# A transformer forward kernel on one core: four small transfers change queue and the mixer around them is re-ordered; the first feed-forward entry is re-cut

## What is computed

```
x = x + sliding_window_sink_attention(rms_norm(x, norm_mix), ...)
x = x + swiglu_ffn(rms_norm(x, norm_ffn), w_gate_up, w_down)      # silu(h @ gate) * (h @ up) @ down
x = rms_norm(x, final_norm)
# the plain mixer, ab_mixer(rms_norm(x, ab_norm)):
p = h @ w_in                       # qk | va | oa | gates (16 columns) | uv
qk = silu(centred_dwconv(qk, conv_w))            # five taps along the sequence
g = gates + gate_b                 # log_i, log_sigmoid(forget), forward and backward
h_fwd, h_bwd = mlstm_scan(q, k, v, ...)          # decay rows from cumulative sums and maxima of g
u, vb = split(gelu(uv));  vb = rms_norm(vb);  hb = u * (ws @ vb + bs)
out = concat(rms_norm(h_fwd + h_bwd) * sigmoid(oa), hb) @ w_out
```

## Time and profile before

| | |
|---|---|
| median of 3 runs | 880.72 us (879.99 to 880.95) |
| the profiled execution | 878.9 us, span 877.2 us |
| TensorE busy | 858.1 us, 98% of the span |
| VectorE, ScalarE, GpSimd busy | 541.6, 434.5, 48.1 us |
| chain that ended last | 92% TensorE, 4% VectorE |
| mean granted TensorE clock | 0.994 |

### The profile page before, as it was taken

How to read it: one execution, slowest core, us unless ns; L and a number is a source line. 1 busy time by engine, 2 the same in 40 slices (tenths; PEclk the granted TensorE clock), 3 DMA queues, 4 the chain that set the end, 5 groups by cost and what they waited for, 6 DMA issues and landing times.

```text
span 877.2 us, 14208 instructions
## 1 busy us (share of the span) xinstructions
PE 858.1 (98%) x5784; PEld 774.5 (88%) x5784; DVE 541.6 (62%) x590; ACT 434.5 (50%) x595; POOL 48.1 (5%) x113
## 2 busy tenths in 40 slices
PE   8999999999999989999999999999999999999996
PEld 8977899999998988889999999999867999999995
DVE  5897554444448669777765555567576675555553
ACT  6675443343344785553744444436465364444431
POOL 2200000000001100310000000003000000000000
PEclk9999999999999998999999999999999999999999
DMA  9644355545555655337575555453602576555601
GB/s 314 226 155 147 121 182 190 193 156 191 188 192 148 221 164 174 115 98 216 177 247 183 184 187 189 135 169 105 230 1 91 195 229 195 181 184 183 190 38 49
DMA packets 98442, 147.68 MB, mean 168 GB/s; under 512 B 4042, under 2 KB 81938, under 8 KB 98402
## 3 DMA queue, kind: packets, MB, share of 16 engines
q1 hardware_dynamic: 97234, 143.11, 50.0%
q0 software_dynamic: 1120, 4.00, 1.6%
q10 hardware_dynamic: 48, 0.02, 0.0%
HBM read 146.05 MB, written 1.05 MB: 168 GB/s over the span
## 4 chain that ended last, share of the span: by engine, by line
PE 92%; DVE 4%; ACT 1%; POOL 1%; issue 1%; DMA 1%; ACTq 0%; DVEq 0%; POOLq 0%
PE bank L1921 28%; PE bank L1922 27%; PE bank L1923 27%; PE bank L1992 1%; PE bank L2579 1%; PE bank L2602 1%; PE bank L2564 1%; PE bank L2558 1%; PE bank L2121 1%; PE bank L2140 1%; DMA x_norm<-arena 1%; DVE w_lo L1209 1%; PE bank L2332 0%; PE bank L2304 0%; PE bank L2044 0%
## 5 line engine op out<-in xcount | busy, mean ns | idle before, releaser
L1209 DVE TENSOR_TENSOR w_lo<-w_raw,w_hi 128x2048 fp32r<-128x2048 f32 (+3 forms) x129 | 289.5, 2252 | 150.9 <-ACT w_hi L682 150.7
L1921 PE MATMUL bank<-xT_hi,w_hi 128*128 128x256 f32 x1068 | 306.0, 286 | 4.3 <-DVE w_lo L1209 4.2
L1923 PE MATMUL bank<-xT_hi,w_lo 128*128 128x256 f32 x1068 | 304.0, 285 | 0.0
L1922 PE MATMUL bank<-xT_lo,w_hi 128*128 128x256 f32 x1068 | 304.0, 285 | 0.0
L682 ACT ACTIVATE w_hi<-w_raw 128x2048 fp32r<-128x2048 f32 (+3 forms) x129 | 241.2, 1877 | 92.4 <-PE bank L1923 85.2
L1921 PEld LDWEIGHTS bank<-xT_hi,w_hi 128*128 128x128 f32 x1068 | 205.6, 192 | 9.3 <-DVE w_lo L1209 4.4
L1922 PEld LDWEIGHTS bank<-xT_lo,w_hi 128*128 128x128 f32 x1068 | 205.7, 193 | 1.9 <-issue 0.2
L1923 PEld LDWEIGHTS bank<-xT_hi,w_lo 128*128 128x128 f32 x1068 | 205.6, 193 | 0.2
L1921 PE MATMUL bank<-w_hi,ff_hi 128*128 128x512 f32 x344 | 134.8, 392 | 0.0
L1922 PE MATMUL bank<-w_lo,ff_hi 128*128 128x512 f32 x344 | 134.5, 391 | 0.0
L1923 PE MATMUL bank<-w_hi,ff_lo 128*128 128x512 f32 x344 | 134.0, 390 | 0.0
(11 more groups left out here) (269 smaller groups left out, 768.6 us busy)
## 6 DMA issues: line engine op xcount, KB each, us to landing
w_raw<-in_ffn_w SPq DMA_DIRECT2D x64, 1024.0 KB, 5.4
w_raw<-in_ffn_w_gate_up SPq DMA_DIRECT2D x22, 1024.0 KB, 5.1
w_raw<-in_ab_w_in SPq DMA_DIRECT2D x12, 1024.0 KB, 6.1
w_raw<-in_ffn_w_down SPq DMA_DIRECT2D x11, 1024.0 KB, 5.0
w_raw<-in_swa_w_in SPq DMA_DIRECT2D x5, 1024.0 KB, 10.9
w_raw<-in_swa_w_out SPq DMA_DIRECT2D x4, 1024.0 KB, 6.3
w_raw<-in_ab_w_out SPq DMA_DIRECT2D x4, 1024.0 KB, 4.9
w_raw<-in_c_w_out SPq DMA_DIRECT2D x4, 1024.0 KB, 6.6
```

The costliest lines, as they stand in the source:

```text
L1209: dve.tensor_tensor(view(w_lo, ch), view(w_raw, ch), view(w_hi, ch).bitcast(F32), ALU.subtract).then_inc(S["lo_done"], 1)
L1921: pe.matmul(out, sh, mh, start=first, stop=False)
L1922: pe.matmul(out, sh, ml, start=False, stop=False)
L1923: return pe.matmul(out, sl, mh, start=False, stop=last)
```

## The change

In the plain mixer the four gate-row transfers are issued by POOL. ACT takes the second half of vb right after the first and rounds C7 and C8 in one go. DVE subtracts C5 to C8 in one go before it waits for the gate rows, does `conv(0)` ahead of `gate_rows`, and spreads C9 to C12 anew. ACT's Exp and Ln move behind its copies of P5.

In the first feed-forward entry DVE subtracts the second chunk in two halves, one ahead of each `normalise`; both row-tile-0 halves are transposed and lowered in one step; T1 is done in halves inside the second visit; and the pieces of the output projection change places, so that the bank of tile 0 ends one piece earlier.

```
+            pool.wait_ge(S["g_raw_ready"], 1)
+            for k in range(4):
+                pool.dma_start(g4[:, k, :], g_raw[4 * k:4 * k + 4, :]).then_inc(S["g4_loaded"], 16)
...
                 sum_squares(n, 0)
-                transposed_high(use, 0, (0,))
-                sum_squares(n, 1, (0,))
-                transposed_high(use, 0, (1,))
-                sum_squares(n, 1, (1,))
-                high_upto(early)
+                transposed_high(use, 0)
+                sum_squares(n, 1)
                 transposed_high(use, 1)
...
             spatial_values(0)
-            act.wait_ge(S["mm_done"], c[3].index + 1)
+            spatial_values(1)
             high_upto(c[6].index + 1)
...
-            act.wait_ge(S["g_raw_ready"], 1)
-            for k in range(4):
-                act.dma_start(g4[:, k, :], g_raw[4 * k:4 * k + 4, :]).then_inc(S["g4_loaded"], 16)
             act.wait_ge(S["pads_ready"], 1)
             act.wait_ge(S["params_ready"], 1)
-            high_upto(c[7].index + 1)
-            spatial_values(1)
-            act.wait_ge(S["g_abs_ready"], 1)
-            step(act.activation(g_w, g_w, ACT.Exp))
-            act.activation(g_w, g_w, ACT.Ln, bias=1.0).then_inc(S["g_ln_ready"], 1)
+            high_upto(c[8].index + 1)
...
+            def enter(use, n, second, then):
+                def part(half):
+                    dve.wait_ge(S["hi_done"], second.index + 1)
+                    k = slice(4 * half, 4 * half + 4)
+                    return dve.tensor_tensor(view(w_lo, second)[:, k], view(w_raw, second)[:, k],
+                                             view(w_hi, second)[:, k].bitcast(F32), ALU.subtract)
...
                 add_residual(n, 0)
-                low_upto(early)
+                part(0)
                 normalise(n, 0, x_norm)
                 add_residual(n, 1, (0,))
-                transposed_low(use, 0, (0,))
+                transposed_low(use, 0)
                 add_residual(n, 1, (1,))
-                transposed_low(use, 0, (1,))
+                part(1).then_inc(S["lo_done"], 1)
+                split[0] += 1
                 normalise(n, 1, x_norm)
...
-            low_upto(c[6].index + 1)
+            low_upto(c[8].index + 1)
...
-            low_upto(c[7].index + 1)
+            conv(0)
...
             gate_rows()
-            for i in range(4):
-                conv(i)
-                low_upto(c[min(8 + i, 10)].index + 1)
+            low_upto(c[9].index + 1)
+            conv(1)
+            low_upto(c[10].index + 1)
...
-            low_upto(c[8].index + 1 + SLOTS)
+            conv(2)
+            conv(3)
+            low_upto(c[11].index + 1)
...
             weighted_scores(1)
+            low_upto(c[12].index + 1)
...
+            swa_values(3)
             out_part(2, 0, 0)
-            swa_values(3)
             out_part(2, 0, 1)
-            out_part(2, 1, 0)
             out_part(3, 0, 0)
             out_part(3, 0, 1)
+            out_part(2, 1, 0)
             out_part(2, 1, 1)
...
-            enter(1, 1, [by_tile(c[0], halves(0)), by_tile(c[1], halves(1))])
+            first, second = by_tile(c[0], halves(0)), by_tile(c[1], halves(1))
+            first(0, low_count=4 + 1)
+            second(0, at=((4, lambda: transpose_tile(1, 1, (0,))), (6, lambda: transpose_tile(1, 1, (1,)))))
+            first(1, low_count=4 + 3)
+            second(1)
```

More of the change, by code:

```diff
@@ L722, in transposed_high, with enter @@
                                    bank[2 * t + half][:], ACT.Copy).then_inc(S["xTh_ready"], 1)
-            def enter(use, n, early, then):
+            def enter(use, n, then):
                 sum_squares(n, 0)
-                transposed_high(use, 0, (0,))
-                sum_squares(n, 1, (0,))
-                transposed_high(use, 0, (1,))
-                sum_squares(n, 1, (1,))
-                high_upto(early)
+                transposed_high(use, 0)
+                sum_squares(n, 1)
                 transposed_high(use, 1)
@@ L833, in _ @@
             c = sched["ffn1"]
-            enter(1, 1, 0, c[3].index + 1)
+            enter(1, 1, c[3].index + 1)
             def silu_gate(ch, i, it=0):
@@ L958, in _ @@
                 last.then_inc(S["conv_begun"], 1)
+                if i == 0:
+                    act.wait_ge(S["g_abs_ready"], 1)
+                    step(act.activation(g_w, g_w, ACT.Exp))
+                    act.activation(g_w, g_w, ACT.Ln, bias=1.0).then_inc(S["g_ln_ready"], 1)
                 high_upto(ch.index + 1 + SLOTS)
@@ L1467, in first_hidden_low @@
                                   ff_hi[0][:].bitcast(F32), ALU.subtract).then_inc(S[ready], 1)
-            enter(1, 1, c[1].index + 1, c[3].index + 1)
+            enter(1, 1, c[1], c[3].index + 1)
             dve.wait_ge(S["ff1_sg"], 1)
```

## The result

The changed kernel takes 869.51 us (median of 4 runs, 868.01 to 869.93); the kernel before, measured beside it, 880.36 us (878.09 to 880.95). The ratio is 0.9878, 95% interval 0.9857 to 0.9900. The prediction said 872.7 us, with a range of 870.8 to 876.5: right in direction, and 1.3 us too slow at the nearer end.

What follows compares the result with a forecast made beforehand. TensorE, busy 858.1 of 877.2 us, was taken as the bound, so only its waits and clock count. Entry 2.1 us plus mixer 5.9 us, 8.0 us off the median, gave 872.7 us, range 870.8 to 876.5.

Steps and rivals of the forecast that it cites:

- The entry, T0: First feed-forward entry: tile 0's bank ends one piece earlier, TensorE's wait shrinks from 2.04 to 0.67 us, gain 1.37 us.
- the halving: First feed-forward entry: the second chunk's subtraction in two halves, the first in VectorE's 3.2 us gap; it costs nothing.
- The entry, T1: First feed-forward entry: transposes of row tile 1 in halves cost 0.86 us against 1.60, gain 0.74 us.
- The mixer: Plain mixer: P8's wait goes (4.38 us) and P8 runs at full clock (1.49 us), together 5.87 us at P9's start.
- The transfers: Plain mixer: four gate-row transfers issued by POOL, the last landing between 315.4 and 318.0, taken as 316.2.
- starved or serial issues: Two mixer rivals: issues waiting for subtractions, 875.1 to 877.7 us, chance 0.07; transfers one behind the other, 891.6 or 881.3, 0.04.
- both slow stretches gone: Plain mixer rival: P10's slow clock stretch goes too, 7.3 us gained in the mixer, 871.3 us, chance 0.20.
- vb came 1.5 us ahead of TensorE: Plain mixer, spatial mixing: vb ready at 351.3, TensorE there at 352.83, so no new wait.
- The sum of 8.0 us: Whole kernel: entry 2.1 us plus plain mixer 5.9 us; 870.9 from the profiled execution, 872.7 from the median.

Runs made afterwards that it cites:

- the pieces alone: The kernel before with only the new order of the pieces of the attention's output projection: 877.30 us, ratio 0.9978.
- the mixer alone: The kernel before with only the edits of the plain mixer, without those of the first feed-forward entry: 872.82 us, ratio 0.9933.

## Why the prediction was off, step by step

**The entry, T0: too small, the step that failed.** It took the distance from the second addition to `normalise` as fixed and moved it up by one piece. That move came as written (1.36 us in the run with the pieces alone, 1.37 predicted). But the distance held 1.2 us (1.51 - 0.30) of GpSimd being locked out by the very subtraction that the change halves, and the halving was costed at nothing because it sits in a gap of VectorE. The row of GpSimd in that gap was not read. Measured: the distance falls from 3.82 to 2.76 us, T0's wait goes from 2.04 to 0, not to 0.67, and the halving is worth 1.04 us.

**How waits were counted.** The profile counts a wait from the modelled end of the last product, 0.39 us after its start, while such products start 0.23 us apart when nothing holds them. So T0 started 88.69 - 86.26 = 2.43 us behind the last product where 0.23 was possible, and the whole wait was worth 2.20 us, not 2.04. The 1.37 us of the prediction are a difference between two waits and don't suffer from this.

**The entry, T1: right, a little small.** Two halves cost 0.44 us each, as predicted (0.43). The prediction compared unlike ends, though: the halves up to the second product behind them, the whole block only up to the first (1.60). Up to the second it is 1.68. So the gain is 1.68 - 0.88 = 0.80 us, 0.74 predicted.

**The entry, the first visit: left out.** Before, the thirteenth product of the first visit, the first that needs the second half of row tile 0, starts 0.11 us late (92.69 behind 92.46, where a step is 0.12), and the one behind it another 0.10. With both halves transposed and lowered in one step this is gone: 0.21 us. T0 itself is 0.20 us shorter (0.79 us to its first product, not 0.98), which belongs to the halving: the run with the whole subtraction has 0.98 again. Together 2.20 + 0.20 + 0.21 + 0.80 = 3.41 us, against 3.42 in the timelines and 2.1 predicted.

**The mixer: right, with one agreement by luck.** 5.87 us predicted at P9, 5.90 measured; the wait and the clock both went, as the windows show. The transfers were sized from 512 KB (4.2 to 6.8 us) and took 2.3; they didn't set anything, since VectorE was in C8's subtraction until 312.8. The rivals with starved or serial issues fell with the row at 306.84. The one with both slow stretches gone did not occur in the profile, but by the mean clock in one of four executions (868.01 us, 0.998). That vb came 1.5 us ahead of TensorE, as worked out, is luck. VectorE's timeline, the product over vb before, then the weighted scores ahead of it after:

```profile
355.98 1.21 DVE L1617 TENSOR_TENSOR arena<-arena 128x1024 f32<-128x1024 f32 x1
```

```profile
345.98 1.15 DVE L1612 SCALAR_TENSOR_TENSOR arena<-bank,arena 128x256 f32<-128x256 f32 x4 [4.19 <-PE bank L2328]
```

The lead was the same before (358.70 - 357.19 = 1.51, and 349.77 - 348.26 = 1.51 after). The product over vb stands in VectorE's queue behind the weighted scores, and these wait for TensorE's own scores. So it follows TensorE, and not the chain over the convolutions, Silu and GpSimd's factor, which ended at 346.31, 0.74 us ahead of it.

**The starting point: wrong.** The sum of 8.0 us was taken from the median of three runs, 880.72, though the profiled execution, on which every term rests, was 878.9. The repeats put the kernel before at 878.97. Its executions lie in two groups: 35 with a mean clock of 0.993 to 0.995 took 878.0 to 879.7 us, 23 with 0.990 to 0.992 took 879.2 to 881.8. The three of the median, 880.0 to 880.95, have the times of the second group; their clocks are not known. The medians of the two groups, 878.8 and 880.3, lie 1.5 us apart, about what the slow stretch behind T0's wait cost in the profile of the mixer alone (1.44). That the second group has this stretch is likely, not shown; if it has, the change removes it together with the wait.

From the profiled execution the sum gives 870.9, and with the measured entry 869.6. So of the 3.2 us of error 1.8 are the starting point and 1.3 the entry; 0.1 remains, less than the start of the kernel varies. The range failed by the same two steps, since none of its cases let a term be larger than written, apart from the clock.

## What to carry to other kernels

Where an engine's tiny operation stands on the chain, read its duration and not only who waited for it: the same instruction at 1.5 us here and 0.3 us there was the sign of a lock-out, and the cure lay in what ran beside it: halving the other instruction, moving it, or feeding it from PSUM each brought the short time back or near it (0.44, 0.19 and 0.30 us). A gap of one engine that "hides" work is only free if the engine whose work fills the gap is not slowed by it. Take a sum from the execution in which its terms were read, and look at the mean clock of the others before trusting a median of three. Compare traces over stretches between the starts of the same two instructions: such stretches agreed to 0.1 us here where nothing in them was changed and the clock stayed up, while executions of the kernel before lay up to 3.8 us apart.

## What the runs showed of the hardware

- A VectorE subtraction with both operands in SBUF holds up a GpSimd operation that reads SBUF until it ends: 0.30 us became 1.51, and 0.19 became 2.16. With one operand in PSUM it didn't (0.30).
- Four 4 KB transfers issued by GpSimd beside such a subtraction were not held up: 2.06 us for the four issues, 2.3 us each to landing. One issue took 0.61 us beside a subtraction and 0.61 us with none running (line 550 at 95.65, kernel before).
- A wait of TensorE of 1.1 us left its granted clock at 1.00, one of 4.2 us was followed by 0.54. One of 2.04 us, at T0, was followed by 1.00 in two profiles of the kernel before and by 0.50 (from 89 to 92 us) in that of the mixer alone. So the length of the wait does not settle it alone.
- The same kernel has executions with and without one more slow stretch: after at 868.01 (mean clock 0.998) and 869.5 to 869.9 (0.995 to 0.996). Such a stretch cost 1.4 us at T0 and 1.5 us in P10. What decides it stays open.
